# Attention in head pairs with split, stacked float32r operands and probabilities scaled on GpSimd

## What is computed

```python
s_c = jnp.einsum('bqghd,bngd->bghqn', qg, k_cmp)
p_c = masked_softmax(s_c, cmp_end[None, :] <= tq[:, None])
o_c = jnp.einsum('bghqn,bngd->bqghd', p_c, v_cmp)
imp = jnp.einsum('bghqn,nj->bgqj', p_c, overlap)        # summed over the heads of a group
_, idx = lax.top_k(score, n_sel)                        # score: imp, forced blocks, validity
p_s = masked_softmax(s_s, mask_s)                       # s_s: queries on the selected keys
p_w = masked_softmax(s_w, mask_w)                       # s_w: queries on the last 512 keys
o = gc[..., 0:1] * o_c + gc[..., 1:2] * o_s + gc[..., 2:3] * o_w
```

## Time and profile before

| | us |
|---|---|
| three runs, median (lowest, highest) | 3602.28 (3601.93, 3602.37) |
| the profiled execution, first to last instruction | 3600.1 |
| attention, tile 0's first to tile 7's last chain step | 712.4 |
| PE busy in those 712.4 | 673.9 |
| DVE, ACT, POOL busy in them | 454.8, 387.9, 0 |

### The profile page before, as it was taken

One profiled execution on the slowest core, in us unless ns is written; L12 is line 12 of the kernel. 1 busy time (PEld: TensorE's weight loads), 2 busy tenths in 40 slices (PEclk: granted clock), 3 DMA queues, 4 the chain that ended last, 5 costly groups with the idle time before them and its releaser, 6 DMA issues.

```text
span 3600.1 us, 42673 instructions
## 1 busy us (share of the span) xinstructions
PE 3400.8 (94%) x16738; PEld 2750.8 (76%) x16738; DVE 1516.6 (42%) x2597; ACT 1263.7 (35%) x2039; POOL 68.5 (2%) x199
## 2 busy tenths in 40 slices
PE   6999987899999999999999999999966999999998
PEld 4778876777887787788888887777854788888886
DVE  5432237766656343442342443274266332212223
ACT  4542125555555422231221223274433231313131
POOL 0000000000000010000000000010000000000000
PEclk9999998999999999999999999999977999999999
DMA  3111320000000141111111113100100211111111
GB/s 119 41 40 60 106 82 1 1 1 1 1 1 1 39 164 47 41 47 53 47 47 49 50 53 110 41 1 18 42 18 1 94 41 47 52 47 47 48 51 64
DMA packets 46249, 163.21 MB, mean 45 GB/s; under 512 B 6096, under 2 KB 7376, under 8 KB 45728
## 3 DMA queue, kind: packets, MB, share of 16 engines
q1 hardware_dynamic: 37152, 126.55, 10.8%
q0 software_dynamic: 8960, 34.77, 2.5%
HBM read 144.53 MB, written 16.78 MB: 45 GB/s over the span
## 4 chain that ended last, share of the span: by engine, by line
PE 76%; DVE 6%; ACT 2%; issue 1%; DMA 0%; POOL 0%; DVEq 0%; ACTq 0%
PE PS L223 52%; PE PS L754 6%; PE PS L727 5%; PE PS L741 3%; PE PS L1360 2%; PE PS L240 2%; PE PS L1336 2%; PE PS L1349 1%; PE PS L775 1%; PE PS L763 1%; DVE SST L1658 1%; DVE SST L1654 1%; PE PS L262 0%; PE PS L1503 0%; DVE AMT L1638 0%
## 5 line engine op out<-in xcount | busy, mean ns | idle before, releaser
L201 DVE TENSOR_TENSOR WLO<-RAW,WHI 128x1024 fp32r<-128x1024 f32 x220 | 269.4, 1225 | 1325.2 <-ACT WHI L196 1325.2
L196 ACT CAST WHI<-RAW 128x1024 fp32r<-128x1024 f32 x220 | 231.4, 1052 | 1635.6 <-PE PS L223 1604.9
L223 PE MATMUL PS<-HHI,WHI 128*128 128x512 f32 x2176 | 679.4, 393 | 5.5 <-DVE W L1112 3.6
L223 PE MATMUL PS<-HLO,WHI 128*128 128x512 f32 x2176 | 671.0, 390 | 0.0
L223 PE MATMUL PS<-HHI,WLO 128*128 128x512 f32 x2176 | 670.4, 389 | 0.0
L223 PEld LDWEIGHTS PS<-HHI,WHI 128*128 128x128 f32 x2176 | 407.5, 188 | 97.8 <-issue 9.0
L223 PEld LDWEIGHTS PS<-HHI,WLO 128*128 128x128 f32 x2176 | 408.9, 188 | 85.4
L223 PEld LDWEIGHTS PS<-HLO,WHI 128*128 128x128 f32 x2176 | 408.8, 188 | 85.4
L223 PE MATMUL PS<-HID_HI,WHI 128*128 128x512 f32 x864 | 266.7, 390 | 2.1 <-DVE HID_LO L1121 2.1
L223 PE MATMUL PS<-HID_LO,WHI 128*128 128x512 f32 x864 | 266.7, 390 | 0.0
L223 PE MATMUL PS<-HID_HI,WLO 128*128 128x512 f32 x864 | 266.4, 390 | 0.0
(11 more groups left out here) (308 smaller groups left out, 4191.5 us busy)
## 6 DMA issues: line engine op xcount, KB each, us to landing
RAW<-in_w SPq DMA_DIRECT2D x220, 512.0 KB, 3.5
X<-in_x SPq DMA_DIRECT2D x8, 512.0 KB, 6.1
merged<-W POOLq DMA_DIRECT2D x8, 512.0 KB, 3.5
gate<-W POOLq DMA_DIRECT2D x8, 512.0 KB, 5.0
W<-gate POOLq DMA_DIRECT2D x8, 512.0 KB, 3.9
W<-merged POOLq DMA_DIRECT2D x8, 512.0 KB, 4.6
X<-in_x POOLq DMA_DIRECT2D x8, 512.0 KB, 9.9
x_kept<-X POOLq DMA_DIRECT2D x8, 512.0 KB, 8.3
```

What stands on the lines that cost most here:

```text
L196: nc.scalar.copy(WHI[:, slot, :], RAW[:, slot, :]).then_inc(w_hi, 1)
L201: nc.vector.tensor_tensor(WLO[:, slot, :], RAW[:, slot, :], WHI[:, slot, :].bitcast(F32), ALU.subtract).then_inc(w_lo, 1)
L223: last = nc.tensor.matmul(o[:, half], w[:, slot, cols], x(k)[:, half], start=(k == 0 and w is WHI and x is hi), stop=(k == kcs - 1 and w i ...
```

## The change

- **Keys.** The rotated keys of both branches go to one tile `KF`. ACT rounds each group's 64 rows to float32r and DVE takes what is left, each twice, so that `KHD[g]` holds the high part of group g's keys on both halves of the partitions and `KLD[g]` the low part on both. Four copies of 2048 columns on ACT (t = 3, 4) and four subtractions on DVE (t = 4, 5) come in; the four memsets and two copies go.
- **Queries.** Per segment ACT rounds the group's queries of the tile (8 heads, 1024 columns, 64 rows) to `QS`, and DVE writes the remainder on the other 64 rows. Issued one segment ahead, in the first pair of a segment.
- **Scores.** Each piece is two float32r products, `QS` on `KHD` and `QS` on `KLD`, accumulated: (high + low) x high + (high + low) x low.
- **Pairs.** Two heads of a group make a pair. A turned chunk is two key tiles of both heads (four blocks, as before); a value product takes one key tile and both heads, 256 columns. There are two output tiles in PSUM, and rounding and remainder of the output take 64 x 256. The compressed scores go through one of the two banks of transposes, from which ACT copies them to SBUF.
- **Order.** Scores of a pair's first head are issued at the start of the pair before it (long) or two before it (short), those of the second head after the first value chunk. Shifts, exponentials and inverses follow. Probability buffers: four in long tiles, six in short ones. The selection work is in pair 1 (short) or 2 (long).
- **Scaling.** DVE only inverts the sums; `pool_probs` scales the probabilities on GpSimd, two instructions a head, in place. POOL does this before `pool_merge`.
- **Places.** The attention's high output goes to `O_HI` in the place of the queries, and the merged tile `MHI` to the place of `HHI`.

```diff
-    KS = [sb("KS0", [T], R + 32 * KB), sb("KS1", [T], R + 40 * KB)]
-    KW = [sb("KW0", [T], R + 36 * KB), sb("KW1", [T], R + 44 * KB)]
-    KCR, VCR = KS[1], KW[1]
+    KF = sb("KF", [2, T], R + 32 * KB)
+    KCR, VCR = sb("KCR", [T], R + 40 * KB), sb("VCR", [T], R + 44 * KB)
...
+    KHD = [sb(f"KHD{g}", [2, T], X_AT + 16 * KB + 8 * KB * g, F32R) for g in range(N_GROUPS)]
+    KLD = [sb("KLD0", [2, T], R + 56 * KB, F32R), sb("KLD1", [2, T], R + 40 * KB, F32R)]
+    QS = [sb(f"QS{i}", [HPG, P], X_AT + 4 * KB * i, F32R) for i in range(2)]
+    half_of = lambda g: slice(HEAD * g, HEAD * g + HEAD)
+    def act_keys_hi(act, g, other):
+        act.wait_ge(rope_done, len(ROPE))
+        act.wait_ge(hid_mm, 2)
+        nc.scalar.copy(KHD[g][half_of(1 - g if other else g), :, :], KF[half_of(g), :, :]).then_inc(k_hi, 1)
+    def dve_keys_lo(dve, g, other):
+        dve.wait_ge(k_hi, 2)
+        nc.vector.tensor_tensor(KLD[g][half_of(1 - g if other else g), :, :], KF[half_of(g), :, :],
+                                KHD[g][half_of(g), :, :].bitcast(F32), ALU.subtract).then_inc(k_lo, 1)
+    def act_queries_hi(act, s):
+        rows, qt = half_of(s % 2), s // 2
+        act.wait_ge(rope_done, len(ROPE))
+        if s >= 2:
+            act.wait_ge(s_done, 2 * HPG * (s - 1))
+        nc.scalar.copy(QS[s % 2][rows, :, :], Q[rows, :, P * qt:P * qt + P]).then_inc(q_hi, 1)
+    def dve_queries_lo(dve, s):
+        rows, qt = half_of(s % 2), s // 2
+        dve.wait_ge(q_hi, s + 1)
+        nc.vector.tensor_tensor(QS[s % 2][half_of(1 - s % 2), :, :], Q[rows, :, P * qt:P * qt + P],
+                                QS[s % 2][rows, :, :].bitcast(F32), ALU.subtract).then_inc(q_lo, 1)
...
-            nc.vector.memset(KS[1][0:HEAD, :], 0.0)
-            nc.vector.memset(KW[1][0:HEAD, :], 0.0)
-            dve.wait_ge(kz_copied, 2)
-            nc.vector.memset(KS[0][HEAD:P, :], 0.0)
-            nc.vector.memset(KW[0][HEAD:P, :], 0.0).then_inc(kz_done, 1)
...
+        if t in (4, 5):
+            for g in range(N_GROUPS):
+                dve_keys_lo(dve, g, t == 5)
...
-            nc.scalar.copy(KS[1][HEAD:P, :], KS[0][HEAD:P, :]).then_inc(kz_copied, 1)
-            nc.scalar.copy(KW[1][HEAD:P, :], KW[0][HEAD:P, :]).then_inc(kz_copied, 1)
+        if t in (3, 4):
+            for g in range(N_GROUPS):
+                act_keys_hi(act, g, t == 4)
+        if t == 5:
+            act_queries_hi(act, 0)
...
+    P_LONG = [sb(f"P_LONG{i}", [T + 5 * P], H_AT + 6656 * i) for i in range(4)]
+    P_SHORT = [sb(f"P_SHORT{i}", [T], H_AT + 4 * KB * i) for i in range(6)]
+    PT = [sb(f"PT{i}", [4, P], W_AT + 12 * KB + 2 * KB * i) for i in range(4)]
+    O_HI = sb("O_HI", [HPG, T], R, F32R)
...
-        return [t[i:i + 4] for i in range(0, len(t), 4)]
+        return [t[i:i + 2] for i in range(0, len(t), 2)]
...
+        s, pair, e = n // HPG, n % HPG // 2, n % 2
+        return s, s // 2, s % 2, 4 * (pair % 2) + 2 * e + pair // 2
+    def heads_of(m):
+        first = where(2 * m)[3]
+        return slice(first, first + 3, 2)
...
+        if m + 2 < PAIRS_SHORT:
+            return m + 2
+        return m + 1 if PAIRS_SHORT <= m + 1 < PAIRS_ALL else None
+    def waits_for_all(m):
+        return m + 1 == PAIRS_SHORT
+    def exp_after(m, chunks):
+        return [chunks - 1] * 4 if waits_for_all(m) else [min(i, chunks - 1) for i in (1, 1, 2, 3)]
...
     def pe_scores(pe, n):
         s, qt, g, j = where(n)
-        q = Q[:, j, P * qt:P * qt + P]
-        if not short(n):
-            pe.wait_ge(shifted, 2 * n)
-        elif n >= 2:
-            pe.wait_ge(shifted, 2 * n - 2)
-        k0 = P * max(0, qt - 4)
-        for ps, keys, lo, hi in ((scores_of(n, 0), KS[g], 0, P * qt + P), (scores_of(n, 1), KW[g], k0, P * qt + P)):
+        pe.wait_ge(q_lo, s + 1)
+        for branch in range(2):
+            if not short(n):
+                pe.wait_ge(shifted, 2 * n - 1 + branch)
+            elif n >= 2:
+                pe.wait_ge(shifted, 2 * n - 3 + branch)
+            lo, hi = (P * max(0, qt - 4) if branch else 0), P * qt + P
             for c in range(lo, hi, 512):
-                m = min(512, hi - c)
-                last = nc.tensor.matmul(ps[:, c - lo:c - lo + m], q, keys[:, c:c + m], start=True, stop=True)
+                end = min(c + 512, hi)
+                out = scores_of(n, branch)[:, c - lo:end - lo]
+                nc.tensor.matmul(out, QS[s % 2][:, j, :], KHD[g][:, branch, c:end], start=True, stop=False)
+                last = nc.tensor.matmul(out, QS[s % 2][:, j, :], KLD[g][:, branch, c:end], start=False, stop=True)
             last.then_inc(s_done, 1)
 
-    def pe_turn(pe, n, i):
-        qt = where(n)[1]
-        c = turned_at[n] + i
+    def pe_turn(pe, m, i):
+        qt = qt_of(m)
+        c = turned_at[m] + i
+        if c >= 2:
+            pe.wait_ge(pt_copied, c - 1)
         for x, (branch, kt) in enumerate(chunks_of(qt)[i]):
-            if (branch, kt) in ((0, 0), (1, max(0, qt - 4))):
-                pe.wait_ge(p_done, 2 * n + branch + 1)
-            if x == 0 and c >= 2:
-                pe.wait_ge(pt_copied, c - 1)
-            src = probs_of(n, branch)
-            col = P * (kt if branch == 0 else kt - max(0, qt - 4))
-            last = nc.tensor.transpose(T_PS[c % 2][:, P * x:P * x + P], src[:, col:col + P], IDENT[:, :])
+            first = max(0, qt - 4) if branch else 0
+            if kt == first:
+                pe.wait_ge(p_done, 4 * m + 3 + branch)
+            for e in range(2):
+                src = probs_of(2 * m + e, branch)[:, P * (kt - first):P * (kt - first) + P]
+                last = nc.tensor.transpose(T_PS[c % 2][:, P * (2 * x + e):P * (2 * x + e) + P], src, IDENT[:, :])
         last.then_inc(t_done, 1)
 
...
+    def pe_use(pe, m, i):
+        chunk = chunks_of(qt_of(m))[i]
+        pe.wait_ge(pt_copied, turned_at[m] + i + 1)
+        u = used_at[m] + i
+        for x, (branch, kt) in enumerate(chunk):
+            last = nc.tensor.matmul(O_PS[m % 2], (VS, VW)[branch][:, kt, :], PT[u % 4][:, 2 * x:2 * x + 2, :],
+                                    start=False, stop=(u + 1 == used_at[m + 1] and x == len(chunk) - 1))
+        last.then_inc(pv_done, 1)
+    def pe_cmp_values(pe, m):
+        s, pair = m // PAIRS, m % PAIRS
         pe.wait_ge(pt_copied, c_turned_at[s] + 1)
-        if n:
-            pe.wait_ge(o_free, n)
-        nc.tensor.matmul(O_PS, VCZ[j % 2][:, :], PCT[s % 2][:, j // 2, :], start=True, stop=False)
-        for i in range(1, len(chunks)):
-            if not short(n):
-                pe_turn(pe, n, i)
-            use(i - 1)
-        use(len(chunks) - 1)
+        if m >= 2:
+            pe.wait_ge(o_free, m - 1)
+        x = 2 * (pair % 2)
+        nc.tensor.matmul(O_PS[m % 2], VCZ[pair // 2][:, :], PCT[s % 2][:, x:x + 2, :], start=True, stop=False)
...
+        for m in range(PAIRS_ALL):
+            s, ahead, chunks = m // PAIRS, ahead_of(m), len(chunks_of(qt_of(m)))
+            if ahead:
+                pe_scores(pe, 2 * ahead)
+            if m % PAIRS == 0 and s + 1 < SEGS:
                 pe_cmp_scores(pe, s + 1)
-            if h == (4 if short(n) else 5) and s + 1 < SEGS:
+            if m % PAIRS == 2 and s + 1 < SEGS:
                 pe_cmp_turn(pe, s + 1)
-            if short(n + 1):
-                for i in range(len(chunks_of(where(n + 1)[1]))):
-                    pe_turn(pe, n + 1, i)
-            pe_values(pe, n)
+            pe_turn(pe, m, 0)
+            if chunks > 1:
+                pe_turn(pe, m, 1)
+            pe_cmp_values(pe, m)
+            pe_use(pe, m, 0)
+            if ahead and not waits_for_all(m):
+                pe_scores(pe, 2 * ahead + 1)
+            for i in range(1, chunks):
+                if i + 1 < chunks:
+                    pe_turn(pe, m, i + 1)
+                pe_use(pe, m, i)
+            if ahead and waits_for_all(m):
+                pe_scores(pe, 2 * ahead + 1)
...
+    def act_cmp_scores(act, s):
+        c = c_scored_at[s]
+        act.wait_ge(t_done, c + 1)
+        nc.scalar.copy(EC[:, :, :], T_PS[c % 2].rearrange("p (h n) -> p h n", n=HEAD)).then_inc(pt_copied, 1)
 
...
+        for m in range(PAIRS_ALL):
+            s, ahead, chunks = m // PAIRS, ahead_of(m), len(chunks_of(qt_of(m)))
+            if m % PAIRS == 0 and s + 1 < SEGS:
+                act_cmp_scores(act, s + 1)
+                act_queries_hi(act, s + 1)
+            if m % PAIRS == 2 and s + 1 < SEGS:
+                act_cmp_copy(act, s + 1)
+            for i in range(chunks):
+                act_copy(act, m, i)
+                if i == 0 and m:
+                    act_out_hi(act, m - 1)
+                for x, after in enumerate(exp_after(m, chunks)):
+                    if ahead and i == after:
+                        act_exp(act, 2 * ahead + x // 2, x % 2)
+            if m % PAIRS == 0 and s + 1 < SEGS:
+                act_cmp_exp(act, s + 1)
+        act_out_hi(act, PAIRS_ALL - 1)
...
+    def dve_shift(dve, n, branch):
```

(118 more changed lines are left out.)

149 lines of the change are left out of this document (53 added, 96 removed).

## The result

The changed kernel takes 3512.62 us (median of 4 runs, 3510.59 to 3513.83), the kernel before, run beside it, 3602.11 (3600.34 to 3602.37): a ratio of 0.975, 95% interval 0.9737 to 0.9764. It is 89.5 us faster; the forecast was 64.3 (3538), and the range held the time. The profiled execution took 3512.54 us, 1.8 more than its span; I had put 2.2 for that distance.

A forecast was written before the change was run, and what follows sets the result against it. PE was taken to bound tiles 4 to 7, a chain through the engines to set tile 0's pace. 3602.3 less 43.6 (tiles 4 to 7) and 21 (tiles 0 to 3) gave 3538 us; range 3508 to 3590.

The forecast's parts named there:

- pairs of 9, 9, 4.9 and 4.9 us: Tile 1: times of a segment's four pairs, the stage taking 2x(9+9+4.9+4.9) = 55.6 us.
- For 128 columns ... I take 0.447: Score remainders of 128 columns: two float32r products priced at 0.447 us, the float32 price of that shape.
- rival (a): Narrow float32r scores are cheap too: 128 columns at 0.22 us, 18 us plus 1.5 in tile 0, 3518; chance 0.24.
- I add 0.3 a pair for the first copy's wait: Tiles 4 to 7: PE's wait for ACT's first copy adds 0.3 us to each pair.
- 2.17+2.5: Tiles 4 to 7, each segment: 1.73+0.44 us for compressed scores and their transposes, and 2.5 us for a new stall.
- Rival (b): Cold first tiles: PE may fall to 1.2 GHz through tiles 0 and 1, adding 26 us, 3564; chance 0.13.
- Hidden, with 0.6 over: Tile 7: POOL's scalings end at 14.1 us, before the next pair's first transpose at 14.7 us.
- Narrower tiles have more room: POOL's scaling in tiles narrower than tile 7: more cover; tile 3 needs 5.5 of 7.7 us.
- Rival (d): POOL becomes the bound: next pair's first transpose waits for scaled probabilities; at 5 ns a column 3681 us; chance 0.07.
- The query split: First pair of a segment: splitting 1024 query columns costs 1.05 us on ACT and 1.2 us on DVE.

The follow-up runs named there:

- Experiment 8: Changed kernel with both score products of every 128-column piece run as float32, everything else the same: 3524.35 us, ratio 0.9779.
- Experiment 6: Changed kernel with the query split done one segment earlier, the first two segments' splits before the attention: 3490.47 us, ratio 0.969.
- experiment 5: Changed kernel with every POOL scaling done twice (doubled) or three times (tripled), extras into an unread tile: 3539.49 us and 3707.11 us.

## Why the prediction was right, and where it was off

**Where the time would go: right.** PE bounds tiles 4 to 7 and a chain the short ones, and before and behind the attention little moved (2.2 us less, 2.6 more). Tiles 0 to 3 came out at 48.5, 56.6, 62.5 and 74.9 us against 49, 55.6, 63.4 and 71.8: 19.9 saved, 21 forecast. The totals agree better than their parts. In tile 1 I had pairs of 9, 9, 4.9 and 4.9 us. From each pair's compressed value product to the next they take 4.8, 10.7, 6.4 and 6.3 us, the last with the next segment's compressed scores in it, so the second pair is the long one. Two readings were slightly off without changing the sum: ACT is busy for 54% of tiles 4 to 7, and ten instructions in 1.14 us make 0.228 us a product.

**Tiles 4 to 7: right mechanism, two terms too dear.** 69.9 us saved, 43.6 forecast. Two terms failed. *"For 128 columns ... I take 0.447"*: the pair of products takes 0.17 us, or 0.22 where another of 512 columns follows (whose first instruction then takes 0.28 instead of 0.23). I had priced it by the shape's nearest row, which was of another type, though the only row with the right type, 512 columns, pointed the other way. Experiment 8 puts the worth of this on the path at 11.7 us, of the 19.5 that rival (a) gave it. *"I add 0.3 a pair for the first copy's wait"*: it is 0.07 now; 32 pairs make 7 us. I read that as the pair order, which puts other work of PE between the first transposes and that copy's use; it wasn't tested alone. With the narrow products at the forecast's price (experiment 8) tiles 4 to 7 still take 13.5 us less than forecast; the copy's wait is 7 of them, and some 6 stay unexplained. The rest of a segment was sized well: tile 4 takes 87.1 us, and eight pairs of 9.78 (808.96 to 818.74) leave 4.4 a segment, where I had 2.17+2.5.

**Rival (a) is what the scores did.** The Trainium skill (FP8 and Floating Point Precision, TensorE Precision Notes) knows no width for the reduced form's speed, and the trace agrees from 512 down to 128 columns: 0.23, 0.17 (384 columns in tile 6), 0.12 (256 columns in tile 5) and 0.06 us for the first instruction of each. The 0.12 and 0.17 are what I had taken from 512 by width.

**Rival (b): its cause came, its cost didn't.** The granted clock of tile 0 fell from 0.82 to 0.75 and of tile 1 from 0.97 to 0.88, but the stages held their forecasts. Experiment 6 brought tile 0 back to 0.82.

**POOL: hidden, but for another reason than the sum gave.** *"Hidden, with 0.6 over"* was worked out for 2.5 ns a column. POOL takes 0.84 ns and 0.34 us, and is waited for 0.2 us. At a price close to the forecast's (experiment 5, doubled) 27 us are lost, so that step of the sum was wrong, and it was luck that POOL is cheap. At tile 7 the doubled scaling costs 4.3 us a head, where the sum had 2.66+1.70, and the stage grew by 4 us instead of staying hidden; and *"Narrower tiles have more room"* was wrong for the long tiles: tile 4 grew most, by 10, where a doubled head costs 3.7 us and 2.5 ns a column and 0.1 us make 3.4. Rival (d)'s place was right and its price too low as well: tripled, by that kernel's own mean durations, a head costs 6.8 us at tile 7, 4.1 ns a column, and 6.1 at tile 4, 4.7 ns, and the kernel takes 3707 us, past the 3681 that I gave for 5 ns. I had added up one pass of a pair and not what a late scaling does to the next pair's scores; that this is what was missing is the untested reading of experiment 5, and PE's lower clock there may have a share too. The Trainium skill (GPSIMD Engine Reference, Performance versus the Vector engine) measured an addition of two tensors at 1.96 times DVE's time. This scaling reads one tensor, and here it is 875 ns against 607 for 640 columns, 1.44 times as long. The same section's rule to use DVE for elementwise work doesn't decide here, since POOL had nothing else to do; but with DVE not the bound either, the move brought 7 us at most.

**The query split: right in kind, and the largest thing left.** I had counted its 1.05 us on ACT and 1.2 on DVE at the start of each segment; moving it off gave 22 us, of which the profiled execution has 16.5 in the stages, 1.1 for each of the fifteen splits of 2.3 us.
